# A root by reciprocal and Sqrt in place of Ln and Exp, and a modulation split between ScalarE and VectorE, in a four-norm decoder step

## The chip, the cores and the metric

One core of a Trainium2 chip runs the kernel. The metric is the device time of one execution in microseconds; several executions give a median. The profile shows one execution, whose span runs from its first to its last instruction.

## The reference

One inference step of a small decoder: a prompt of 256 tokens and 8 sequences of 4 sample tokens (288 columns in all), model width 1024, two layers. Each layer has two sublayers, each of which begins with the same modulated norm:

```python
def rms_norm(x, g):
    y = xf * lax.rsqrt(jnp.mean(xf * xf, axis=-1, keepdims=True) + RMS_EPS)
    return (y * g).astype(x.dtype)
def modulate(x, g, shift, scale):
    return rms_norm(x, g) * (1 + scale) + shift
...
x += gate * f(modulate(x, ...))     # f: mixer, SwiGLU, pooling mixer, top-2-of-8 MoE
```

Layer 0 has a mixer (attention with forget gates beside an RWKV-7 recurrence) and a dense SwiGLU; layer 1 has a pooling mixer and a mixture of 8 experts. The recurrence's output passes a group norm per head, `(y - mean) * rsqrt(var + GN_EPS)`, before the output projection. Shift, scale and gate come from a conditioning vector through the matrices called ada below; they differ between the prompt (one vector) and the eight sample sequences (one each).

## The kernel before, in words

Everything is float32 and held transposed: the 1024 features lie as 8 chunks of 128 partitions, the tokens along the columns, prompt in 0 to 255 (NP = 256), samples in 256 to 287. `xT`, `hT`, `tmpT` and `yT` (8 chunks x 288 columns each) are parts of one tensor, which the profile calls `wide`.

Each engine runs its own program in the order in which it is written, and semaphores join them. A modulated norm, number i = 0 to 3, goes like this:

- ScalarE squares the 8 chunks of x (`square_all(i)`); TensorE sums them over the partitions with a matrix of ones (`mean_square(i)`), so that each partition holds the sum for each token.
- VectorE, in `mean_of(i)`, turns the sum into mean + eps in `rstd` (128 x 288, line L1864) and gives the semaphore `ms_read`. ScalarE, in `root(i)` by `inverse_root`, takes Ln (L1611) and Exp with a scale of -0.5 (L1612), and gives `rooted`. VectorE then multiplies all of x by `rstd` into `hT` (L1866, 128 x 2304).
- VectorE, in `modulated(i)`, scales and shifts the sample columns in two operations (L1874, L1875, 128 x 256 each) and then the prompt columns chunk by chunk, 8 operations of 128 x 256 with the chunk's gain and shift as one value per partition (L1878). Each of the eight gives one count of `h_ready`.
- TensorE waits for the chunks one by one: norm 0 before the input projection, norm 1 before the SwiGLU's first gate matrix, norm 3 before the router. Norm 2 is used by VectorE (a copy into `ext`, L2197, and the window sums), by GpSimd and by TensorE, which all wait for its 8 chunks.

In norm 0 the mean and the multiply by `rstd` come early on VectorE, while TensorE still works on the first four ada matrices; the gain and shift (`mod_tile`, `gains(0)`) come later, and `modulated(0)` after them.

The group norm uses the same `inverse_root` on 128 x 1152: three operations of VectorE write variance + eps into `tmpT` (L2138), ScalarE takes Ln and Exp, and VectorE multiplies (L2142), scales and shifts (L2145), adds a bonus (L2146) and multiplies by a gate (L2148), whose end gives `mix_ready`, for which the output projection and the loads of the next weights wait.

Functions of ScalarE belong to table sets. Where the next function is in another set than the one loaded, the build puts an ACT_TABLE_LOAD ahead of it. The other uses of `inverse_root` (q and k norm, the recurrence's key norm) stay as they are.

Of the kernel before, what the change touches and what calls it, by code (L numbers as in the profile page):

```python
# [20 lines left out]
ALU = mybir.AluOpType  # L21
ACT = mybir.ActivationFunctionType
# [3 lines left out]
D = 1024  # L26
DC = D // P
NP, NB, NT = 256, 8, 4
NS = NB * NT
N = NP + NS  # L30
# [3 lines left out]
HC = HW // P  # L34
# [131 lines left out]
class Named:  # L166
# [5 lines left out]
    def __call__(self, name):  # L172
        if name not in self.made:
# [5 lines left out]
ONCE = {  # L179
    "vector": ("vec_copied vec2_copied k_ready q_ready last_ready rp_mixed lf_abs lf_one logf_ready negF_ready "  # L180
              "kk_scaled rk_ready cum_ready psm_shifted psm_ready delta_ops packed final_state gn_centred "
              "mix_ready exts_zero ext_done picked top_ready placed planned numbered weighted y2 y0 y1"),
    "scalar": ("siluc c_copied qk_squared qk_rooted lf_exp lf_ln wl_tanh gl_sigmoid kk_squared kk_rooted "
              "psm_exped so_copied fst_copied syt_copied gn_squared gn_rooted gate_spread top_exped scaled2 scaled0 scaled1"),
    "tensor": ("c_turned vec_turned vec2_turned lf_turned last_turned so_mm fst_mm syt_mm route_mm rank_mm"),
# [39 lines left out]
def spread(ap, axis, n):  # L225

    ap = ap.unsqueeze(axis)
    shape = list(ap.shape)
    shape[axis] = n
    return ap.to_broadcast(shape)  # L230


def flat(t):
    return t[:, :, :].rearrange("p a b -> p (a b)")
# [46 lines left out]
def build_program(nc, a, y_p, y_s, k_p, k_s, v_p, v_s, lf_p, lf_s, st_p, st_s, sh_p, sh_s, pool_p, pool_s):  # L281

    ctx = ExitStack()
    with ctx:
# [3 lines left out]
        s = Named(nc, ctx)  # L288
        once = Once(s)

        def sums(name, which, n):

            return s(f"sums_{which}"), 3 * ("kks", "bon", "gnm", "gnv").index(name) + n
# [236 lines left out]
            return first, out  # L530

        cumv = winv

        def sample_operands():

# [570 lines left out]
        def _(pe):  # L1106
# [67 lines left out]
            for i, (_, wd, chunks) in enumerate(WIN):  # L1174
                w = tile(TILES.index(("win", i)))[:, 0:DC * wd].rearrange("p (c f) -> p c f", c=DC)
                for kind, idx, off, m in chunks:
                    b = banks.open(pe, f"win{n}", (s("win_act" if n % 2 else "win_dve"), n // 2 + 1))
                    for c in range(DC):
                        if n == 0:
                            pe.wait_ge(s("h_ready"), c + 1)  # L1180
                        last = mm(b[0:m, 0:N], w[:, c, off:off + m], hT[:, c, :], c == 0, c == DC - 1)
                    last.then_inc(s("win_mm"), 1)
                    n += 1
                if i == 2:
                    pe.wait_ge(s("vec2_loaded"), 16 * len(others))
                    b = banks.open(pe, "vec2", once("vec2_copied"))
                    for k in range(2):
                        last = pe.transpose(b[:, P * k:P * (k + 1)], vrow[:, 1 + k, :], ident)
                    last.then_inc(once.give("vec2_turned"), 1)
                if i == 4:  # L1190
                    pe.wait_ge(*once("qk_squared"))
                    for k in range(6):
                        b = banks.open(pe, f"qkms{k}", (s("qkms_read"), k + 1))
                        mm(b[:, 0:384], K("pairs"), flat(tmpT)[:, 384 * k:384 * (k + 1)], True, True).then_inc(s("qkms"), 1)
                if i:
                    fold(0, 3 + i)
                ada(0, 4 + i)
# [278 lines left out]
            def hidden(i):  # L1476
                nf = FGRP[i][1]
                for j in range(nf // P):
                    for kind in ("gate", "up"):
                        w = tile(TILES.index((kind, i)))[:, 0:DC * nf].rearrange("p (c f) -> p c f", c=DC)  # L1480
                        n = 4 * i + j
                        b = banks.open(pe, f"{kind}{n}", (s("act_ready"), n + 1))
                        for c in range(DC):
                            if i + j == 0 and kind == "gate":
                                pe.wait_ge(s("h_ready"), DC + c + 1)
                            last = mm(b[:, 0:N], w[:, c, P * j:P * (j + 1)], hT[:, c, :], c == 0, c == DC - 1)
                        last.then_inc(s(f"{kind}_mm"), 1)

# [30 lines left out]
                last = pe.transpose(b[:, 120 * c:120 * (c + 1)], prow[0:120, P * (4 + c):P * (5 + c)], ident[0:120, 0:120])  # L1519
            last.then_inc(s("pb_mm"), 1)  # L1520

            pe.wait_ge(s("h_ready"), 3 * DC)
            for half in range(2):
                b = banks.open(pe, f"hl{half}", (s("hl_copied"), half + 1))
                for c in range(4):
# [25 lines left out]
            for blk, (t0, w) in enumerate(BLK):  # L1551
                for c in range(DC):
                    if blk == 0:
                        pe.wait_ge(s("h_ready"), 3 * DC + c + 1)
                    last = mm(b[0:w, NE * blk:NE * (blk + 1)], hT[:, c, t0:t0 + w], routerw[:, c, :], c == 0, c == DC - 1)
            last.then_inc(once.give("route_mm"), 1)
            for n in range(6):
# [27 lines left out]
        def _(act):  # L1585
# [23 lines left out]
            def inverse_root(v, sem):  # L1609

                me.step(act.activation(v, v, ACT.Ln), chain)  # L1611
                me.give(act.activation(v, v, ACT.Exp, scale=-0.5), sem)  # L1612

            def root(i):
                act.wait_ge(s("ms_read"), i + 1)
                inverse_root(rstd[:, :], s("rooted"))

            square_all(0)
            root(0)
# [1 line left out]
            def ada(layer, i):  # L1621
                k = 12 * layer + i
                act.wait_ge(s("ada_mm"), k + 1)
                if k >= 2:
                    act.wait_ge(s("folded"), k - 1)
                copy(adap[layer][:, k % 2, :], banks[f"ada{layer}_{i}"][:, :], s("ada_copied"))

            for i in range(4):
                ada(0, i)

            def proj_chunk(n):
                kind, idx, _, m = WCHUNKS[n]
# [136 lines left out]
            copy(yT[:, HC:2 * HC, NP:N], banks["syt"][:, 0:HC * NS].rearrange("p (c t) -> p c t", c=HC), once.give("syt_copied"))  # L1769
            act.wait_ge(*once("gn_centred"))  # L1770
            me.give(act.activation(flat(tmpT)[:, 0:HC * N], flat(yT)[:, HC * N:2 * HC * N], ACT.Square), once.give("gn_squared"))  # L1771
            act.wait_ge(*sums("gnv", "read", 3))
            inverse_root(flat(tmpT)[:, 0:HC * N], once.give("gn_rooted"))


            square_all(1)
            root(1)
            for n in range(FF // P):
                act.wait_ge(s("gate_mm"), n + 1)
                if n >= 2:  # L1780
                    act.wait_ge(s("act_ready"), n - 1)
                me.give(act.activation(ffsilu[:, n % 2, :], banks[f"gate{n}"][:, 0:N], ACT.Silu), s("silu_ready"))
                if n >= 4 and (n % 4 == 3 or n == FF // P - 1):
                    ada(1, 2 * (n // 4) - 2)
                    ada(1, 2 * (n // 4) - 1)
# [4 lines left out]
            for half in range(2):  # L1790
                act.wait_ge(s("pb_mm"), half + 1)
                act.wait_ge(*once("exts_zero"))
                me.give(act.activation(exts[:, 4 * half:4 * half + 4, :, 1:16],
                                       banks[f"pb{half}"][:, 0:480].rearrange("p (c b r) -> p c b r", c=4, r=PBUF),
                                       ACT.Copy), s("pbuf_copied"))
            for half in range(2):
                act.wait_ge(s("hl_mm"), half + 1)
                copy(hlast[0:NS + 16, 512 * half:512 * (half + 1)], banks[f"hl{half}"][0:NS + 16, :], s("hl_copied"))
# [6 lines left out]
                copy(dst[0:w, 512 * (n % 2):512 * (n % 2 + 1)], banks[f"gr{n}"][0:w, :], s("hl_copied"))  # L1805
            square_all(3)
            root(3)
            act.wait_ge(*once("ext_done"))
            for n in range(6):
                w = BLK[n // 2][1]  # L1810
# [19 lines left out]
        def _(dve):  # L1830
# [4 lines left out]
            def do(ins, sem=None):  # L1835
                me.step(ins, sem or chain)
# [24 lines left out]

            def mean_of(i):
                dve.wait_ge(s("ms_ready"), i + 1)
                do(TS(rstd[:, :], banks[f"ms{i}"][:, 0:N], 1.0 / D, RMS_EPS, ALU.mult, ALU.add), s("ms_read"))  # L1864
                dve.wait_ge(s("rooted"), i + 1)
                do(TT(hT[:, :, :], xT[:, :, :], spread(rstd[:, :], 1, DC), ALU.mult))  # L1866

            def by_seq(ap):
                return ap.rearrange("p c (b t) -> p c b t", t=NT)

            def modulated(i):

                hs = by_seq(hT[:, :, NP:N])
                do(TT(hs, hs, spread(gainT[i][:, :, 1:9], 3, NT), ALU.mult))  # L1874
                do(TT(hs, hs, spread(mod(i, 0)[:, :, 1:9], 3, NT), ALU.add))  # L1875
                for c in range(DC):
                    v = hT[:, c, 0:NP]
                    me.give(TS(v, v, gainT[i][:, c, 0:1], mod(i, 0)[:, c, 0:1], ALU.mult, ALU.add), s("h_ready"))  # L1878

# [256 lines left out]
            for i in range(3):  # L2136
                dve.wait_ge(*sums("gnv", "mm", i + 1))
                do(TS(flat(tmpT)[:, 384 * i:384 * (i + 1)], banks[f"gnv{i}"][:, 0:384], 1.0 / DH, GN_EPS, ALU.mult, ALU.add),  # L2138
                   s("sums_read"))
            dve.wait_ge(*once("gn_rooted"))  # L2140
            r = flat(tmpT)[:, 0:HC * N]
            do(TT(y2, y2, r, ALU.mult))  # L2142
            for c in range(HC):
                v = yT[:, HC + c, :]
# [48 lines left out]
            do(dve.memset(ext[:, :, 0:16], 0.0))  # L2193
            mean_of(2)
            modulated(2)
            dve.wait_ge(s("h_ready"), 3 * DC)
            do(dve.tensor_copy(ext[:, :, 16:16 + NP], hT[:, :, 0:NP]))  # L2197
            for lv in range(4):
                a0, a1 = (ext, ext2) if lv % 2 == 0 else (ext2, ext)
# [44 lines left out]
        def _(pool):  # L2244
# [93 lines left out]
            pool.wait_ge(s("mix_stored"), 16 * len(stores))  # L2338
            me.step(pool.memset(tables, 0.0), once.give("tables_zero"))

            pool.wait_ge(s("h_ready"), 3 * DC)
            pool.wait_ge(s("pbuf_copied"), 2)
            hs = by_sequence(hT[:, :, NP:N])
            me.step(pool.tensor_copy(exts[:, :, :, 16:20], hs), s("pool_chain"))
# [137 lines left out]
```

## Time and profile before

| | |
|---|---|
| median of 3 runs | 2011.12 us (2007.43 to 2011.98) |
| the profiled execution | 2009.45 us, span 2007.6 us |
| TensorE matmuls busy | 1770.9 us, 88% of the span |
| VectorE, ScalarE, GpSimd busy | 424.8, 241.3, 167.3 us |
| ACT_TABLE_LOADs ahead of L1611 and L1612 | 7 and 7, 1283 ns each |

The busy share of an engine is over the whole span; what a change in one place is worth is read from the engines' rows around that place. In the rows, "idle before" is the time an engine stood still before an instruction, and the arrow names what ended it.

### The profile page before, as it was taken

What the parts mean: (1) busy time and instruction counts of PE and PEld (TensorE: products, weight loads), DVE (VectorE), ACT (ScalarE), POOL (GpSimd) and SP (SyncE); (2) the same over time, 40 slices, a digit from 0 to 9 for tenths busy, and PEclk for the clock granted to TensorE, in tenths of its full rate; (3) what the DMA queues carried; (4) which work ended last, traced back from release to release, by engine and by line L of the source; (5) the groups of instructions that cost most, each with busy time, mean ns of one, the idle gap of its engine ahead of it and who ended that gap; (6) DMA issues with size and microseconds to landing.
All of it is one profiled execution on the core that took longest, in us unless ns stands there. A gap on an engine that the chain in (4) does not pass through costs nothing.

```text
span 2007.6 us, 27180 instructions
## 1 busy us (share of the span) xinstructions
PE 1770.9 (88%) x10676; PEld 1295.1 (65%) x10677; DVE 424.8 (21%) x794; ACT 241.3 (12%) x489; POOL 167.3 (8%) x201
## 2 busy tenths in 40 slices
PE   6999886566789999967889999999999999999874
PEld 3766444555567777745339789788777887778331
DVE  2023435965211111275000000000000000000102
ACT  2022242111110000132000000001000010000101
POOL 4002203562000000040000000000000000000001
PEclk8999597666899999978999999999999999999997
DMA  9762042000745554530898868869999999999995
GB/s 342 269 231 88 2 127 57 1 1 27 249 169 210 210 189 159 190 133 2 315 391 325 304 252 319 302 252 354 363 345 345 346 348 352 343 348 367 367 392 211
DMA packets 235294, 481.64 MB, mean 240 GB/s; under 512 B 16575, under 2 KB 90691, under 8 KB 234803
## 3 DMA queue, kind: packets, MB, share of 16 engines
q1 hardware_dynamic: 229755, 471.92, 65.2%
q0 software_dynamic: 3904, 5.44, 0.9%
q10 hardware_dynamic: 1568, 3.34, 0.5%
q8 instruction: 48, 0.79, 0.2%
q14 instruction: 19, 0.16, 0.0%
HBM read 473.13 MB, written 7.90 MB: 240 GB/s over the span
## 4 chain that ended last, share of the span: by engine, by line
PE 78%; DMA 7%; DVE 5%; POOL 4%; issue 3%; ACT 2%; SPq 2%; ACTq 0%; POOLq 0%; DVEq 0%
PE bank L1108 76%; DMA ring<-in_moe_w_up 4%; POOL ring L2301 2%; DMA ring<-in_ada_w 1%; POOL other L2310 1%; ACT ring L1590 1%; SPq L2423 1%; SPq L2388 0%; DVE wide L1882 0%; DVE wide L1866 0%; PE bank L1241 0%; SPq L2414 0%; DVE wide L2204 0%; PE bank L714 0%; DMA ring<-in_cache_fox_logf 0%
## 5 line engine op out<-in xcount | busy, mean ns | idle before, releaser
L1108 PE MATMUL bank<-wide,ring 128*128 128x144 f32 (+4 forms) x4240 | 695.6, 331 | 16.6 <-DVE wide L1878 9.3
L1108 PEld LDWEIGHTS bank<-wide,ring 128*128 128x128 f32 (+2 forms) x4240 | 616.5, 191 | 100.3 <-issue 34.9
L1108 PE MATMUL bank<-ring 128*64 128x512 f32 (+8 forms) x1748 | 339.3, 519 | 50.6 <-DMA ring<-in_moe_w_up 24.5
L1108 PE MATMUL bank<-other,ring 128*128 128x144 f32 (+3 forms) x2016 | 292.2, 320 | 50.3 <-POOL ring L2301 29.8
L1108 PEld LDWEIGHTS bank<-other,ring 128*128 128x128 f32 (+1 forms) x2016 | 267.8, 194 | 75.3 <-POOL ring L2301 31.4
L1108 PEld LDWEIGHTS bank<-ring 128*64 128x64 f32 (+4 forms) x1748 | 143.1, 158 | 226.2 <-issue 189.2
L1108 PE MATMUL bank<-ring,other 128*64 128x512 f32 x560 | 128.0, 596 | 8.4 <-ACT other L747 8.4
L820 DVE TENSOR_TENSOR other<-other,bank 64x512 f32<-64x512 f32 (+1 forms) x40 | 24.5, 613 | 441.6 <-ACT other L744 441.6
L838 DVE TENSOR_TENSOR other<-other,bank 128x288 f32<-128x288 f32 (+3 forms) x48 | 21.4, 446 | 350.9 <-PE bank L1108 324.4
L2367 POOL TENSOR_TENSOR small<-const 128x1 f32<-128x1 f32 x1 | 0.2, 193 | 1074.7 <-DMA expert_rows<-ring 1074.7
L1108 PEld LDWEIGHTS bank<-ring,other 128*64 128x64 f32 x560 | 38.4, 137 | 75.4 <-issue 64.3
L1108 PEld LDWEIGHTS bank<-const,other 64*128 64x128 f32 (+2 forms) x408 | 49.3, 182 | 32.3 <-issue 28.2
L744 ACT ACTIVATE other<-bank 64x512 f32<-64x512 f32 (+1 forms) x40 | 21.6, 540 | 394.8 <-PE bank L1108 382.9
L2301 POOL TENSOR_TENSOR ring<-ring,const 64x256 f32<-64x256 f32 x48 | 63.7, 1327 | 55.0 <-DVE ring L2095 46.9
L1590 ACT ACTIVATE ring<-bank 128x512 f32<-128x512 f32 (+8 forms) x110 | 45.0, 436 | 166.6 <-PE bank L1108 114.0
L757 ACT ACTIVATE other<-bank 128x288 f32<-128x288 f32 (+3 forms) x48 | 19.3, 403 | 360.9 <-PE bank L1108 349.0
L1108 PE MATMUL bank<-const,other 64*128 64x64 f32 (+2 forms) x408 | 59.0, 281 | 0.0
L1108 PE MATMUL bank<-ring,silucT 128*32 128x512 f32 x384 | 46.6, 616 | 5.0 <-DMA ring<-in_ada_w 5.0
L1108 PE MATMUL bank<-other 128*128 128x288 f32 (+3 forms) x128 | 43.2, 482 | 5.4 <-DVE other L963 2.6
L1590 ACT ACTIVATE other<-bank 128x512 f32<-128x512 f32 (+4 forms) x48 | 24.3, 525 | 171.4 <-PE bank L1108 149.3
L2165 DVE TENSOR_TENSOR other<-other,bank 128x288 f32<-128x288 f32 x22 | 10.0, 454 | 163.1 <-PE bank L1108 163.1
L1108 PE MATMUL bank<-wide,const 128*128 128x288 f32 (+1 forms) x100 | 36.4, 509 | 7.6 <-ACT wide L1771 3.2
(353 smaller groups left out, 956.5 us busy)
## 6 DMA issues: line engine op xcount, KB each, us to landing
ring<-in_moe_w_gate SPq DMA_DIRECT2D x32, 2048.0 KB, 8.0
ring<-in_moe_w_up SPq DMA_DIRECT2D x32, 2048.0 KB, 12.7
ring<-in_moe_w_down SPq DMA_DIRECT2D x32, 2048.0 KB, 16.8
ring<-in_ada_w SPq DMA_DIRECT2D x24, 2048.0 KB, 13.7
ring<-in_moe_w_gate SPq DMA_DIRECT2D x32, 1536.0 KB, 11.1
ring<-in_moe_w_up SPq DMA_DIRECT2D x32, 1536.0 KB, 14.8
ring<-in_moe_w_down SPq DMA_DIRECT2D x32, 1536.0 KB, 16.5
ring<-in_w_in SPq DMA_DIRECT2D x5, 2048.0 KB, 12.7
```

Source lines behind the costliest of these rows:

```text
L744: act.activation(sg[0:HALF, part, 0:P * n], B[part][HALF:P, 0:P * n], ACT.Silu).then_inc(s("moe_silu"), 2)
L757: act.activation(sg[:, p % 2, 0:w], B[2 * (p % 2)][:, 0:w], ACT.Silu).then_inc(s("moe_silu"), 3 if p == 3 else 1)
L820: dve.tensor_tensor(ea[0:HALF, part, 0:P * n], sg[0:HALF, part, 0:P * n], B[part][0:HALF, 0:P * n], ALU.mult)\
L838: dve.tensor_tensor(eaT[:, 2 * p:2 * p + n, 0:k], sg[:, p % 2, 0:n * k].rearrange("p (c q) -> p c q", c=n), B[2 * (p % 2) + 1][:, 0:n * k] ...
L1108: return pe.matmul(out, lhsT, rhs, start=start, stop=stop, skip_group_check=True)
L1590: me.give(act.activation(out, in_, ACT.Copy), sem)
L2165: do(TT(ffact[:, i % 2, n % 4, :], ffsilu[:, n % 2, :], banks[f"up{n}"][:, 0:N], ALU.mult), s("act_ready"))
L2301: me.step(pool.tensor_tensor(nm[o, n % 2], of(gt[o, n % 2], a_)[:, :, 0:L], mask, ALU.mult), s("nm_ready") if a_ else s("pool_chain"))
L2310: me.step(pool.tensor_tensor(vk, spread(sval[:, t, :], 2, DH), spread(svec[:, t, 3, :], 1, 32), ALU.mult), s("vk_ready"))
L2367: me.step(pool.tensor_tensor(small[:, 50:51], ident[:, 0:1], ident[:, 0:1], ALU.add), s("pool_chain"))
L2423: sp.dma_start(svec[2 * H * q + f:2 * H * (q + 1):2].rearrange("p t i k -> p (t i) k"), scratch[q].rearrange("t i h k -> h (t i) k")).then ...
```

## The change

The diff does three things. In the norms and in the group norm, VectorE takes the reciprocal of mean + eps (or variance + eps) and ScalarE one Sqrt of it; `ms_read` and the new `gn_inverted` are given by the reciprocal. The multiply of x by `rstd` leaves `mean_of` and goes into `modulated`, where it is cut into three: the sample columns, the prompt columns of chunks 0 to 3 (whose end gives `h_scaled`), those of chunks 4 to 7. And ScalarE, in its own `modulated(i)`, scales and shifts the prompt columns of chunks 0 to 3 (Identity with the gain as scale and the shift as bias), while VectorE does chunks 4 to 7. TensorE, VectorE and GpSimd wait for `h_act` or `h_ready` through `modulated_chunk`.

```diff
+        HALF_C = DC // 2
+        def modulated_chunk(i, c):
+            return (s("h_act"), HALF_C * i + c + 1) if c < HALF_C else (s("h_ready"), HALF_C * i + c + 1 - HALF_C)
...
-                            pe.wait_ge(s("h_ready"), c + 1)
+                            pe.wait_ge(*modulated_chunk(0, c))
...
             def root(i):
                 act.wait_ge(s("ms_read"), i + 1)
-                inverse_root(rstd[:, :], s("rooted"))
+                me.give(act.activation(rstd[:, :], rstd[:, :], ACT.Sqrt), s("rooted"))
+            def modulated(i):
+                for c in range(HALF_C):
+                    act.wait_ge(s("h_scaled"), i + 1)
+                    v = hT[:, c, 0:NP]
+                    act.activation(v, v, ACT.Identity, scale=gainT[i][:, c, 0:1], bias=shift_of(i)[:, c, 0:1]).then_inc(s("h_act"), 1)
...
-            act.wait_ge(*sums("gnv", "read", 3))
-            inverse_root(flat(tmpT)[:, 0:HC * N], once.give("gn_rooted"))
+            act.wait_ge(*once("gn_inverted"))
+            me.give(act.activation(flat(tmpT)[:, 0:HC * N], flat(tmpT)[:, 0:HC * N], ACT.Sqrt), once.give("gn_rooted"))
...
             def mean_of(i):
                 dve.wait_ge(s("ms_ready"), i + 1)
-                do(TS(rstd[:, :], banks[f"ms{i}"][:, 0:N], 1.0 / D, RMS_EPS, ALU.mult, ALU.add), s("ms_read"))
+                do(TS(rstd[:, :], banks[f"ms{i}"][:, 0:N], 1.0 / D, RMS_EPS, ALU.mult, ALU.add))
+                do(dve.reciprocal(rstd[:, :], rstd[:, :]), s("ms_read"))
                 dve.wait_ge(s("rooted"), i + 1)
-                do(TT(hT[:, :, :], xT[:, :, :], spread(rstd[:, :], 1, DC), ALU.mult))
...
             def modulated(i):
                 hs = by_seq(hT[:, :, NP:N])
+                do(TT(hT[:, :, NP:N], xT[:, :, NP:N], spread(rstd[:, NP:N], 1, DC), ALU.mult))
                 do(TT(hs, hs, spread(gainT[i][:, :, 1:9], 3, NT), ALU.mult))
                 do(TT(hs, hs, spread(mod(i, 0)[:, :, 1:9], 3, NT), ALU.add))
-                for c in range(DC):
+                for c0, sem in ((0, s("h_scaled")), (HALF_C, chain)):
+                    do(TT(hT[:, c0:c0 + HALF_C, 0:NP], xT[:, c0:c0 + HALF_C, 0:NP], spread(rstd[:, 0:NP], 1, HALF_C), ALU.mult), sem)
+                for c in range(HALF_C, DC):
                     v = hT[:, c, 0:NP]
                     me.give(TS(v, v, gainT[i][:, c, 0:1], mod(i, 0)[:, c, 0:1], ALU.mult, ALU.add), s("h_ready"))
...
+            r = flat(tmpT)[:, 0:HC * N]
+            do(dve.reciprocal(r, r), once.give("gn_inverted"))
             dve.wait_ge(*once("gn_rooted"))
-            r = flat(tmpT)[:, 0:HC * N]
             do(TT(y2, y2, r, ALU.mult))
```

ScalarE's `modulated(0)` stands after its copies for the first four ada matrices, `modulated(1)` and `modulated(3)` right after their `root`, `modulated(2)` after `root(2)` and two copies into `exts`.

## Rows read from the trace of the kernel before

**Rows 1.** The page's chain that ended last, shares of the span by engine
```profile
PE 78%; DMA 7%; DVE 5%; POOL 4%; issue 3%; ACT 2%; SPq 2%; ACTq 0%; POOLq 0%; DVEq 0%
```

**Rows 2.** Waits of TensorE, 44 to 120 us: total, times, longest
```profile
PE bank L1108 <- DVE wide L1878: 2.3, 1, 2.3
```

**Rows 3.** Windows: stretch, length, busy (instructions) of PE, PEld, DVE, ACT, POOL, clock, DMA
```profile
45.50:50.00 4.50, 4.46 (x10) 3.21 (x11) 2.15 (x7) 0.00 (x0) 0.00 (x0) 0.50 1.05 387
...
560.00:854.00 294.00, 294.00 (x1357) 220.07 (x1358) 42.27 (x109) 19.29 (x41) 0.00 (x0) 0.99 0.51 183
```

**Rows 4.** Timeline, norm 1: start, duration, engine, line, operation, [idle before, releaser]
```profile
552.91 0.46 DVE L1864 TENSOR_SCALAR rstd<-bank 128x288 f32<-128x288 f32 x1 [2.95 <-PE bank L1108]
553.40 0.44 ACT L1611 ACTIVATE rstd<-rstd 128x288 f32<-128x288 f32 x1 [1.66 <-DVE rstd L1864]
553.86 1.28 ACT L1612 ACT_TABLE_LOAD   x1
555.15 0.44 ACT L1612 ACTIVATE rstd<-rstd 128x288 f32<-128x288 f32 x1
...
555.70 2.56 DVE L1866 TENSOR_TENSOR wide<-wide,rstd 128x2304 f32<-128x2304 f32 x1 [2.33 <-ACT rstd L1612]
...
559.21 2.67 DVE L1878 TENSOR_SCALAR wide<-wide,gainT,modT 128x256 f32<-128x256 f32 x8
...
559.77 6.47 PE L1108 MATMUL bank<-wide,ring 128*128 128x288 f32 x18 [6.97 <-DVE wide L1878]
```

**Rows 5.** Timeline, the group norm's root
```profile
505.71 0.56 DVE L2138 TENSOR_SCALAR wide<-bank 128x384 f32<-128x384 f32 x1 [0.72 <-PE bank L1108]
...
508.78 1.16 ACT L1612 ACTIVATE wide<-wide 128x1152 f32<-128x1152 f32 x1
510.04 1.36 DVE L2142 TENSOR_TENSOR wide<-wide 128x1152 f32<-128x1152 f32 x1 [3.77 <-ACT wide L1612]
```

**Rows 6.** Timeline, norm 0 (VectorE), and TensorE's first projection matmuls
```profile
26.12 2.56 DVE L1866 TENSOR_TENSOR wide<-wide,rstd 128x2304 f32<-128x2304 f32 x1 [2.33 <-ACT rstd L1612]
...
44.06 0.42 DVE L1874 TENSOR_TENSOR wide<-wide,gainT 128x256 f32<-128x256 f32 x1
...
45.54 18.73 PE L1108 MATMUL bank<-wide,ring 128*128 128x288 f32 x64 [2.32 <-DVE wide L1878]
```

**Rows 7.** Timeline, norms 2 and 3 and the router
```profile
859.43 2.56 DVE L1866 TENSOR_TENSOR wide<-wide,rstd 128x2304 f32<-128x2304 f32 x1 [2.33 <-ACT rstd L1612]
...
865.65 1.23 DVE L2197 COPY other<-wide 128x2048 f32<-128x2048 f32 x1
...
893.78 2.56 DVE L1866 TENSOR_TENSOR wide<-wide,rstd 128x2304 f32<-128x2304 f32 x1 [2.33 <-ACT rstd L1612]
...
897.85 7.92 PE L1108 MATMUL bank<-routerw,wide 128*128 128x8 f32 x48 [6.97 <-DVE wide L1878]
```

**Rows 8.** Small VectorE operations: ns min/median/max, first and last start, shapes
```profile
L1986 DVE RECIPROCAL small<-small x8: 165/166/166, 203.0 to 239.5; 128x2 f32<-128x2 f32 x8
...
L1063 DVE RECIPROCAL low<-low x1: 176/176/176, 935.5 to 935.5; 128x3 f32<-128x3 f32 x1
...
L1040 DVE TENSOR_SCALAR low<-low x1: 153/153/153, 927.4 to 927.4; 128x1 f32<-128x1 f32 x1
...
L994 DVE TENSOR_TENSOR low<-low x1: 159/159/159, 918.0 to 918.0; 128x1 f32<-128x1 f32 x1
```

**Rows 9.** ScalarE by form: busy us, mean ns, idle before; then a timeline row
```profile
L1590 ACT ACTIVATE other<-bank 128x288 f32<-128x288 f32 x17 | 7.0, 410 | 92.2 <-PE bank L1108 92.2
...
L1693 ACT ACTIVATE other<-bank,vT 128x288 f32<-128x288 f32 x8 | 4.0, 498 | 3.0 <-PE bank L1108 3.0
...
L1800 ACT ACTIVATE silucT<-modT 128x256 f32<-128x256 f32 x1 | 0.4, 403 | 0.0
...
16.88 2.77 ACT L1607 ACTIVATE wide<-wide 128x288 f32<-128x288 f32 x8 [6.09 <-DVE wide L1842]
```

**Rows 10.** Timeline, ScalarE's first copy for the experts after the top-2 Exp
```profile
924.07 0.41 ACT L946 ACTIVATE wide<-bank 128x288 f32<-128x288 f32 x1 [7.03 <-PE bank L1108]
```

More of the change, by code:

```diff
@@ L181 @@
               "kk_scaled rk_ready cum_ready psm_shifted psm_ready delta_ops packed final_state gn_centred "
-              "mix_ready exts_zero ext_done picked top_ready placed planned numbered weighted y2 y0 y1"),
+              "gn_inverted mix_ready exts_zero ext_done picked top_ready placed planned numbered weighted y2 y0 y1"),
     "scalar": ("siluc c_copied qk_squared qk_rooted lf_exp lf_ln wl_tanh gl_sigmoid kk_squared kk_rooted "
@@ L532, in build_program, with shift_of @@
         cumv = winv
+        HALF_C = DC // 2
+        def shift_of(i):
+            return modT[i // 2][:, 24 * (i % 2):24 * (i % 2) + 8, :]
+        def modulated_chunk(i, c):
+            return (s("h_act"), HALF_C * i + c + 1) if c < HALF_C else (s("h_ready"), HALF_C * i + c + 1 - HALF_C)
         def sample_operands():
@@ L1484, in hidden @@
                             if i + j == 0 and kind == "gate":
-                                pe.wait_ge(s("h_ready"), DC + c + 1)
+                                pe.wait_ge(*modulated_chunk(1, c))
                             last = mm(b[:, 0:N], w[:, c, P * j:P * (j + 1)], hT[:, c, :], c == 0, c == DC - 1)
@@ L1520, in _ @@
             last.then_inc(s("pb_mm"), 1)
-            pe.wait_ge(s("h_ready"), 3 * DC)
+            for c in (HALF_C - 1, DC - 1):
+                pe.wait_ge(*modulated_chunk(2, c))
             for half in range(2):
@@ L1553, in _ @@
                     if blk == 0:
-                        pe.wait_ge(s("h_ready"), 3 * DC + c + 1)
+                        pe.wait_ge(*modulated_chunk(3, c))
                     last = mm(b[0:w, NE * blk:NE * (blk + 1)], hT[:, c, t0:t0 + w], routerw[:, c, :], c == 0, c == DC - 1)
@@ L1629, in _ @@
                 ada(0, i)
+            modulated(0)
             def proj_chunk(n):
@@ L1771, in _ @@
             me.give(act.activation(flat(tmpT)[:, 0:HC * N], flat(yT)[:, HC * N:2 * HC * N], ACT.Square), once.give("gn_squared"))
-            act.wait_ge(*sums("gnv", "read", 3))
-            inverse_root(flat(tmpT)[:, 0:HC * N], once.give("gn_rooted"))
+            act.wait_ge(*once("gn_inverted"))
+            me.give(act.activation(flat(tmpT)[:, 0:HC * N], flat(tmpT)[:, 0:HC * N], ACT.Sqrt), once.give("gn_rooted"))
             square_all(1)
             root(1)
+            modulated(1)
             for n in range(FF // P):
@@ L1795, in _ @@
                                        ACT.Copy), s("pbuf_copied"))
+            modulated(2)
             for half in range(2):
@@ L1807, in _ @@
             root(3)
+            modulated(3)
             act.wait_ge(*once("ext_done"))
@@ L2195, in _ @@
             modulated(2)
-            dve.wait_ge(s("h_ready"), 3 * DC)
+            for c in (HALF_C - 1, DC - 1):
+                dve.wait_ge(*modulated_chunk(2, c))
             do(dve.tensor_copy(ext[:, :, 16:16 + NP], hT[:, :, 0:NP]))
@@ L2339, in _ @@
             me.step(pool.memset(tables, 0.0), once.give("tables_zero"))
-            pool.wait_ge(s("h_ready"), 3 * DC)
+            for c in (HALF_C - 1, DC - 1):
+                pool.wait_ge(*modulated_chunk(2, c))
             pool.wait_ge(s("pbuf_copied"), 2)
```

## The prediction, as it was put on record

> **What bounds the kernel now.** First the page's chain of work that ended last: 78% of it is TensorE [rows 1], so the norms matter only where TensorE stands still for them. The question for each of the five places that the diff touches (norms 0 to 3, the group norm) is whether the wait there ends last and whether the time is given back later. The waits of TensorE and the timeline answer it. At norm 0 TensorE waits 2.3 us for the first modulated chunk and for nothing else up to 120 us [rows 2], so what is lost there is lost for the projections. At norm 1 it stands still for 6.97 us, and the reader can follow the baton: VectorE's mean, Ln, a table load, Exp, the multiply, two sample operations, the first chunk [rows 4]. After that it works without a gap from 560 to 854 us [rows 3], so no transfer takes the difference up. The group norm's root is the 3.77 us for which VectorE waits while TensorE waits too [rows 5]. Norm 2 feeds VectorE's own chain of window sums, and norm 3 the router, before which TensorE again stands for 6.97 us [rows 7]. All five are on the path, except the first half of norm 0: its multiply ends at 28.68 us, while its gains are ready only at 44.06 [rows 6].
>
> **What is removed.** Ln and Exp cost, from the end of the mean (553.37) to the start of the multiply (555.70), 2.33 us: 0.03 to reach ScalarE, 0.44 Ln, 0.02, a table load of 1.28, 0.44 Exp, 0.11 back [rows 4]. Ln's own load is not in it: ScalarE stood idle for 1.66 us just before Ln, with its table already in. Sqrt takes Ln's place and its load can hide in the same idle time, so I count none for it. The same stretch of the group norm is 3.77 us [rows 5].
>
> On the load, the Trainium skill (ScalarE: Activation LUTs, What ACT_TABLE_LOAD costs) says that a switch costs the 1.28 us load plus a drain of about 1.38. The trace does not show that drain: the load starts 0.02 us after Ln ends, and Exp 0.01 after the load [rows 4]. By the page, four switches off the path would give back 5.5 us more than the rows allow, an estimate that turns a sum of +9.2 into +3.7; it gets no chance of its own, because the rows time this very switch.
>
> **What is added in its place: a reciprocal.** Write r for its time per column in ns and take 0.15 us as its fixed part. The new stretch of a norm is 0.03 + (0.15 + 0.288 r) + 0.03 + 0.44 + 0.11 = 0.76 + 0.288 r, against 2.33: a change of -1.57 + 0.288 r. The group norm: 0.03 + (0.15 + 1.152 r) + 0.03 + 1.16 + 0.10 = 1.47 + 1.152 r against 3.77: -2.30 + 1.152 r. Norms 1, 2 and 3 and the group norm together: -7.0 + 2.02 r. Norm 0's root is covered by the 15 us that VectorE has until its gains; if that cover went, it would cost as much as the others.
>
> So everything hangs on r, and no reciprocal of more than three columns is in the trace. Lower end: the rate of ordinary operations, (2558 - 159) / 2303 = 1.04 ns a column, from the multiplies of 2304 columns and of one [rows 4, 8]. Upper end: two reciprocals of different width, 166 ns at two columns and 176 at three, 10 ns a column [rows 8]. In between: if the fixed part is that of the one-column tensor-scalar (153 less its column, 152), two columns give 7 and three give 8 ns. One column more or less is thin evidence, since fixed parts vary by some nanoseconds from operation to operation; but at the ordinary rate the step from two columns to three should be 1 ns and is 10. I take r = 8, near the steep rows. Then the reciprocal is 2.45 us in a norm and 9.4 in the group norm, and the roots together cost -7.0 + 16.1 = +9.1 us: the norms +0.73 each, the group norm +6.9.
>
> The Trainium skill (VectorE: DVE Perf Modes, First, the fixed hardware budget) says that the reciprocal is an iterative divide on two slices with a repeat count of 8; at that page's 0.96 GHz, if the count is paid per column, that is 8.3 ns, an estimate by which the sum would be +9.9 us instead of the +9.2 below.
>
> **What is moved: the multiply and the split.** After the root, before: multiply, two sample operations (0.46 each with the gap), first chunk, and TensorE starts 4.07 us after the multiply's start in norms 1 and 3 [rows 4, 7]. After: three sample operations, 3 x 0.46 = 1.38; half the prompt, 0.16 + 1024 x 1.04 ns = 1.23, and 0.04 to reach ScalarE; one Identity; 0.14 to TensorE, as now. An Identity of 256 columns with two per-partition operands is not in the trace: a copy of that size takes 0.403, one per-partition operand adds 0.088 (498 against 410 at 288 columns) [rows 9]; with a second, 0.58, taken as 0.60. The first chunk is then there at 3.4 us.
>
> - Norm 1: 3.4 against 4.07, -0.67. At the half clock that TensorE has after such a pause, a matmul takes 0.45 us (ten in 4.46 at granted clock 0.50 [rows 3]). Squares of 288 columns follow each other at 0.33 though one lasts 0.44 [rows 9], so Identities should follow at 0.33 to 0.60, say 0.45: they keep up. At 0.60, three chunks lose 0.45.
> - Norm 0: the multiply now stands behind the gains. Before, 44.06 to 45.54 = 1.48; after, 3.4: +1.92 on the path [rows 6]. This cover is what the edit gives up.
> - Norm 2: VectorE needs all chunks itself, before 865.65 - 859.43 = 6.22 [rows 7]; after, 1.38 + two halves 2.53 + four chunks at 0.33 and a last tail, 1.45 = 5.36: -0.86. ScalarE's four are done by 2.65 + 0.60 + 3 x 0.45 = 4.6, earlier.
> - Norm 3: the router takes a chunk in about 0.33 (24 chunk products of two parts in 7.92 [rows 7]), so ScalarE's pace shows. Before, the first 8 were through at 4.07 + 8 x 0.33 = 6.71; after, 3.4 + 3 x 0.45 + 5 x 0.33 = 6.40: -0.31, between -0.67 and +0.14.
>
> Together +0.08, within -0.4 and +1.0: the split nearly pays for norm 0.
>
> **Costed at nothing.** The top-2 softmax's Exp now finds Sqrt's table and needs its own load, 1.28; ScalarE stands idle for 7.03 us behind it [rows 10], so nothing is late. SwiGLU's Silu load moves behind four Identities; ScalarE has nothing to do until the first gate product, 8 matmuls of 0.36 us or more after TensorE's start [rows 4]. Identity may need a table of its own; its load would fall in the time that ScalarE waits for `h_scaled`. `ms_read` comes later by the reciprocal, and with it a PSUM bank that is next taken eight banks on. No DMA issue is moved; SP's loads after `mix_ready` shift with it.
>
> **Sum.** -7.0 + 16.1 + 0.1 = +9.2 us on the profiled execution's 2009.45 (span 2007.6 and 1.85 around it), 2018.65. The median of the runs is 1.67 above that execution, so the forecast is 2011.12 + 9.2 = 2020.3. In general the sum is -6.9 + 2.02 r: it is zero at r = 3.4, and 0.2% (4.0 us, about what a measurement of this kernel can tell from no change) is passed above 5.4 and below 1.4.
>
> **Rivals.**
> 1. The reciprocal runs at one column a cycle, like the rest. For it: all other VectorE operations do, and 166 against 159 ns at so few columns is no great difference. Against it: the 10 ns step. Then the sum is -6.9 + 2.1 = -4.8, 2006.3 us: faster, by just over 0.2%. It decides wherever r is below 1.4. Chance 0.21. The Trainium skill (Vector Engine (DVE) Microarchitecture Reference, ALU special-value part) has the divide chain span all eight slices, which a pipeline could feed with a column a cycle; no row here shows that.
> 2. A rate between, 2 to 5 ns: 2008.3 to 2014.3 us, no change to be told. For it: fixed part 158, as the one-column multiply has [rows 8], gives 4 and 6. Chance 0.08.
> 3. Sqrt's load is not hidden: it lands behind the wait at the group norm and at norm 2 (norms 1 and 3 find it loaded), +2.6 us on the forecast, 2022.9. Against it: Ln's load, in the same place, was early. Chance 0.03.
> 4. The forecast, r from 5.4 to 10: 2015 to 2025, with the split's bounds. Chance 0.68.
>
> **Range and chances.** The likeliest case has 2015 to 2025.5 for itself. It holds too little alone, so the range goes down to rival 1's time: 2006 to 2025.5, leaving out half of rival 1 and the ends. Slower 0.71 (forecast and rival 3), same 0.16 (rival 2 and the part of rival 1 that falls short of 0.2%), faster 0.13.
>
> **What would show it.** The RECIPROCAL rows of 288 and 1152 columns: 2.45 and 9.4 us here, 0.46 and 1.36 in rival 1. VectorE's idle before the first multiply after a root: 0.60 us instead of 2.33. No table load between the reciprocal and Sqrt. TensorE's start after the gains of norm 0: 3.4 us instead of 1.48; the first Identity 0.60 long. The prediction is wrong if a 288-column reciprocal is under 1.7 us.

## The result, and the profile after

The changed kernel takes 2018.07 us (median of 8 runs, 2014.45 to 2019.70), the kernel before 2010.77 beside it (8 runs, 2007.41 to 2013.45). The medians lie 7.3 us apart. The ratio with its 95% interval, which is the measure from here on, is 1.0028 [1.0015, 1.0040]: slower by 5.6 us (3.0 to 8.0), against a forecast of +9.2 (2020.3 us). The profiled execution took 2018.64 us, its span 2016.8, against 2009.45 and 2007.6.

Line numbers move: L1864 of before is L1886, Ln and Exp of a norm (L1611, L1612) have become the reciprocal L1887 and Sqrt L1627, the first chunks' scale and shift is ScalarE's L1634, and the group norm's multiply L2142 is L2168. VectorE by form, grouped by line (busy us, mean ns of one, idle before), after:

```profile
L1887 DVE RECIPROCAL rstd<-rstd 128x288 f32<-128x288 f32 x4 | 7.8, 1953 | 0.1
L2166 DVE RECIPROCAL wide<-wide 128x1152 f32<-128x1152 f32 x1 | 7.4, 7353 | 0.0
L2011 DVE RECIPROCAL small<-small 128x2 f32<-128x2 f32 x8 | 1.3, 166 | 0.3
L1073 DVE RECIPROCAL low<-low 128x3 f32<-128x3 f32 x1 | 0.2, 175 | 0.0
```

The two wide rows give the unknown of the prediction: (7353 - 1953) / 864 = 6.25 ns a column, and 1953 - 288 x 6.25 = 153 ns fixed. That line passes through the two-column row too (165.5 against 166).

Timeline of norm 1, after, which answers to [rows 4]:

```profile
561.10 0.46 DVE L1886 TENSOR_SCALAR rstd<-bank 128x288 f32<-128x288 f32 x1 [2.95 <-PE bank L1118]
561.59 1.95 DVE L1887 RECIPROCAL rstd<-rstd 128x288 f32<-128x288 f32 x1
563.58 0.44 ACT L1627 ACTIVATE rstd<-rstd 128x288 f32<-128x288 f32 x1 [4.95 <-DVE rstd L1887]
564.12 0.43 DVE L1896 TENSOR_TENSOR wide<-wide,rstd 128x256 f32<-128x256 f32 x1 [0.58 <-ACT rstd L1627]
564.58 0.42 DVE L1897 TENSOR_TENSOR wide<-wide,gainT 128x256 f32<-128x256 f32 x1
565.04 0.42 DVE L1898 TENSOR_TENSOR wide<-wide,modT 128x256 f32<-128x256 f32 x1
565.50 2.48 DVE L1900 TENSOR_TENSOR wide<-wide,rstd 128x1024 f32<-128x1024 f32 x2
566.76 1.58 ACT L1634 ACTIVATE wide<-wide,modT,gainT 128x256 f32<-128x256 f32 x3 [2.74 <-DVE wide L1900]
...
567.50 0.82 PE L1118 MATMUL bank<-wide,ring 128*128 128x288 f32 x1 [6.51 <-ACT wide L1634]
```

No table load stands between reciprocal and Sqrt. From the end of the mean (561.56) to the first multiply (564.12) it is 2.56 us where [rows 4] have 2.33: the root lost 0.23. From there to TensorE's start it is 3.38 where it was 4.07: the split won 0.69. TensorE stands still for 6.51 us instead of 6.97.

Timeline of the group norm's root, after, for [rows 5]:

```profile
504.24 1.28 ACT L1792 ACT_TABLE_LOAD   x1
...
508.25 0.56 DVE L2163 TENSOR_SCALAR wide<-bank 128x384 f32<-128x384 f32 x1 [0.38 <-PE bank L1118]
508.84 7.35 DVE L2166 RECIPROCAL wide<-wide 128x1152 f32<-128x1152 f32 x1
516.23 1.16 ACT L1792 ACTIVATE wide<-wide 128x1152 f32<-128x1152 f32 x1 [10.70 <-DVE wide L2166]
517.49 1.36 DVE L2168 TENSOR_TENSOR wide<-wide 128x1152 f32<-128x1152 f32 x1 [1.30 <-ACT wide L1792]
...
523.55 1.81 PE L1118 MATMUL bank<-wide,other 128*128 128x288 f32 x3 [15.41 <-DVE wide L2174]
```

The load runs while VectorE still waits for the sums. From the end of the last variance to the multiply it is 517.49 - 508.81 = 8.68 us, against 3.77: +4.91, and TensorE waits 15.41 us for the whole chain (10.50 before). This is the largest single loss.

VectorE's timeline, after: first operations behind the gains (norm 0) and behind the roots of norms 2 and 3, for [rows 6, 7]:

```profile
42.43 0.23 DVE L1882 TENSOR_TENSOR gainT<-gainT,vT 128x72 f32<-128x72 f32 x1
42.70 0.42 DVE L1896 TENSOR_TENSOR wide<-wide,rstd 128x256 f32<-128x256 f32 x1
...
868.00 0.42 DVE L1896 TENSOR_TENSOR wide<-wide,rstd 128x256 f32<-128x256 f32 x1 [0.58 <-ACT rstd L1627]
...
873.38 1.23 DVE L2224 COPY other<-wide 128x2048 f32<-128x2048 f32 x1
...
901.75 0.43 DVE L1896 TENSOR_TENSOR wide<-wide,rstd 128x256 f32<-128x256 f32 x1 [0.58 <-ACT rstd L1627]
```

And TensorE's, after: the first projection matmuls, the router, and what follows it:

```profile
46.08 4.18 PE L1118 MATMUL bank<-wide,ring 128*128 128x288 f32 x8 [4.22 <-ACT wide L1634]
...
905.13 8.05 PE L1118 MATMUL bank<-routerw,wide 128*128 128x8 f32 x48 [6.52 <-ACT wide L1634]
913.11 4.84 PE L1572 MATMUL bank<-const,wide 128*128 128x128 f32 x24
...
923.52 6.79 PE L1118 MATMUL bank<-other 128*128 128x288 f32 x27 [1.00 <-DVE other L973]
```

Norm 0 starts the projections 46.08 - 42.70 = 3.38 us behind its gains, 1.90 later than before (1.48). The copy into `ext` starts 5.38 us after the multiply (6.22 before), the router 3.38 (4.07 before).

One table for the whole span, in us: each stretch runs from the milestone before it. "Unchanged" is the kernel before run once more (below).

| stretch | before | unchanged | after | changed again |
|---|---|---|---|---|
| start to gains of norm 0 | 44.02 | 42.80 | 42.66 | 42.38 |
| to the projections' start | 1.52 | 1.52 | **3.42** | **3.42** |
| to the group norm's mean | 453.08 | 453.84 | 455.08 | 451.39 |
| to its multiply | 11.42 | 11.43 | **16.33** | **16.33** |
| to the output projection's start | 6.06 | 6.06 | 6.06 | 6.06 |
| to norm 1's mean | 36.81 | 38.29 | 37.55 | 37.76 |
| to the first gate matmul | 6.86 | 6.86 | **6.40** | **6.40** |
| to norm 2's mean | 296.87 | 297.62 | 297.48 | 297.58 |
| to the copy into `ext` | 9.01 | 9.02 | **8.40** | **8.41** |
| to norm 3's mean | 25.34 | 25.33 | 25.34 | 25.34 |
| to the router's start | 6.86 | 6.87 | **6.41** | **6.41** |
| to the top-8 search | 8.36 | 8.36 | **8.49** | **8.49** |
| to the experts' plan | 21.38 | 21.75 | 22.49 | 22.55 |
| to the experts' first matmul | 25.33 | 25.49 | 25.16 | 25.34 |
| to the end | 1054.68 | 1054.76 | 1055.53 | 1055.54 |

The bold stretches are the edited places. They sum to +1.90 + 4.91 - 0.46 - 0.61 - 0.45 + 0.13 = +5.4 us, and they repeat to 0.01 us. The rest of the 9.2 between the two spans lies in stretches that also differ by up to 1.5 us between the two executions of the unchanged kernel, and by 3.7 (to the group norm's mean) between those of the changed one: run to run, except for the stretch to the plan, which is taken up below.

### The profile page after: what moved, and what is told of

Same layout as the page of the kernel before. It is cut to its first block, busy times and chain, and to the rows that moved or that the text cites. A ratio compares the mean times of both kernels' runs of the same rounds, so it can differ in the third digit from the quotient of the medians.

```text
span 2016.8 us, 27183 instructions
## 1 busy us (share of the span) xinstructions
PE 1774.4 (88%) x10676; PEld 1296.4 (64%) x10677; DVE 436.2 (22%) x791; ACT 239.3 (12%) x494; POOL 167.5 (8%) x201
## 4 chain that ended last, share of the span: by engine, by line
PE 77%; DMA 6%; DVE 6%; POOL 3%; issue 3%; SPq 2%; ACT 2%; ACTq 0%; DVEq 0%; POOLq 0%
PE bank L1118 76%; DMA ring<-in_moe_w_up 4%; POOL ring L2328 2%; DMA ring<-in_ada_w 1%; POOL other L2337 1%; ACT ring L1601 1%; SPq L2451 1%; SPq L2416 0%; DVE wide L1907 0%; DVE wide L2166 0%; PE bank L1251 0%; DVE wide L2231 0%; SPq L2442 0%; DMA ring<-in_cache_fox_logf 0%; DVE wide L1900 0%
## 5 line engine op out<-in xcount | busy, mean ns | idle before, releaser
L848 DVE TENSOR_TENSOR other<-other,bank 128x288 f32<-128x288 f32 (+3 forms) x48 | 21.4, 446 | 350.9 <-PE bank L1118 324.8
```

Source lines behind the costliest of these rows:

```text
L848: dve.tensor_tensor(eaT[:, 2 * p:2 * p + n, 0:k], sg[:, p % 2, 0:n * k].rearrange("p (c q) -> p c q", c=n), B[2 * (p % 2) + 1][:, 0:n * k] ...
```

## The experiments

Theories, stated for all runs: **A**, the reciprocal's rate per column is the whole loss, and the edited rows add up to the time. **B**, the rival: the split, or something behind the rows (ScalarE's pace, the clock of TensorE), takes a share that the rows of the edited places don't show. Ratios are against the kernel before on the same chip, five rounds each, its median beside them.

### Roots alone, and the split alone

```diff
# e1_roots_only: the kernel before, and
-                inverse_root(rstd[:, :], s("rooted"))
+                me.give(act.activation(rstd[:, :], rstd[:, :], ACT.Sqrt), s("rooted"))
...
+                do(dve.reciprocal(rstd[:, :], rstd[:, :]), s("ms_read"))
...   # the same in the group norm
# e2_split_only: the kernel after, with inverse_root in both places and no reciprocal
```

> Reciprocal and Sqrt in the four norms and the group norm, but no split: VectorE multiplies and modulates all chunks as before. If the reciprocals make the loss (1.95 us at 288 columns and 7.35 at 1152 in the profile after), each norm is +0.23 us (0.76 + 1.80 - 2.33) in norms 1 to 3 and the group norm +4.9 (1.47 + 7.20 - 3.77): +5.6 us over the kernel before, about 2016.4. If the loss comes from the split and the moved multiply, this kernel is within 2 us of the one before.

Measured: 2020.08 us against 2010.09, 1.0048 [1.0030, 1.0065]. Its rows: norms 1 to 3 +0.23 each, the group norm +4.94, norm 0 nothing (its projections start 1.52 us after the gains, as before), +5.6 in all. The time says +9.6 (6.0 to 13.1), 4.0 more than the rows.

> The split between ScalarE and VectorE and the moved multiply, but all roots by Ln and Exp as before. Reciprocal theory: norm 0 +1.9, norms 1 to 3 together -1.9 (-0.67, -0.86, -0.31 were forecast), so no change from the kernel before, within 1 us. Split theory: +5 us or more over before.

Measured: 2011.24 against 2010.09, 1.0009 [0.9998, 1.0021]. Its rows: norm 0 +1.90, norms 1 to 3 -0.69, -0.83 and -0.55, together -0.2. The time says +1.8 (-0.4 to +4.2), 2.0 above the rows, which the interval does not resolve. So the loss sits in the roots, as A has it; the excess of e1 over its rows is open.

### The group norm's reciprocal, taken away, doubled, and alone

```diff
# e3_gn_undone: the kernel after, but
-            do(dve.reciprocal(r, r), once.give("gn_inverted"))
...
+            inverse_root(flat(tmpT)[:, 0:HC * N], once.give("gn_rooted"))
# e4_gn_twice: the kernel after, and ahead of its own reciprocal
+            do(dve.reciprocal(flat(tmpT)[:, HC * N:2 * HC * N], r))
# e8_gn_only: the kernel before, and
+            do(dve.reciprocal(r, r), once.give("gn_inverted"))   # and one Sqrt for Ln and Exp
```

> The whole change, except that the group norm's root is Ln and Exp again. Reciprocal theory: 4.9 us faster than the whole change, so +0.8 over before (three norms +0.7, split +0.1). If the group norm's extra time is given back later (the loads after it have more time), it stays within 1.5 us of the whole change, +6 to +7 over before.

Measured: 2013.79 against 2010.09, 1.0020 [1.0009, 1.0030]; the stretch to the group norm's multiply is 11.40 us again, where the kernel after has 16.33. The other edited rows leave +0.5, and the time says +4.0 (1.8 to 6.0), 3.5 above them. That is neither of the two times expected: +0.8 lies outside the interval, and +6 at its edge.

> The whole change with a second reciprocal of 1152 columns into a scratch part ahead of the group norm's own; no result changes. If the time of that instruction passes to the end one to one, +7.35 us over the whole change, about +14 over before. If what follows takes part of it back, less than +5 over the whole change.

Measured: 2024.94 against 2010.09, 1.0077 [1.0062, 1.0092], +15.5 (12.5 to 18.5), 9 to 10 us above what the ratios of the kernel after give (+5.6, and +6.4 below), where +7.35 was expected; the intervals hold that too. VectorE's timeline of it:

```profile
508.58 7.35 DVE L2166 RECIPROCAL wide<-wide 128x1152 f32<-128x1152 f32 x1
515.97 7.35 DVE L2167 RECIPROCAL wide<-wide 128x1152 f32<-128x1152 f32 x1
```

The second copy costs its 7.35 us and the 0.04 between them, all on the path: the stretch to the group norm's multiply is 23.66 us instead of 16.33, and nothing covers the reciprocal. Its edited rows add up to +12.8, and the time lies 2.7 above them.

These four kernels were timed beside one and the same group of runs of the kernel before, and all four lie above their rows, by 4.0, 2.0, 3.5 and 2.7 us. Compared with each other, e4 and e3, which differ in the group norm's root alone, are 11.5 us apart by their ratios and 12.3 by their rows. An offset that the four have in common drops out of that difference, and the two reciprocals show in it nearly whole.

> The kernel before with one edit, the group norm's root by reciprocal and Sqrt. Per-column theory (0.15 us + 6.25 ns a column, 7.35 us at 1152): 1.47 + 7.20 against 3.77, +4.9 us, ratio 1.0024, which is most of the whole change's loss. If the loss is spread over the norms or lies in the split, under +2.

Measured: 2015.93 against 2010.96, 1.0023 [1.0012, 1.0034], +4.6 (2.4 to 6.8), where its one edited stretch has +4.86. Here rows and time agree.

### How large the noise is

The kernel before and the kernel after were run once more (c1_unchanged, c2_changed_again).

> The kernel before once more, as a measure of what two runs of one program differ by, in total and in each stretch between the norms: ratio 1.000 within 0.001 by any theory. If stretches that no edit touches (projection start to group norm, output projection, top-2 to plan) come out 1 to 2 us longer here too than in the first profile of before, their difference in the other kernels is not the change's.

> The changed kernel once more, beside the runs of this chip. The sum over the rows of its edited places is +5.1 us (norm 0 +1.9, group norm +4.6, norms 1 to 3 -1.4); the first timing gave +7.3 between medians. Rows theory: +5 to +6. If the change costs another 2 us in stretches that it doesn't edit: +7 to +8.

Measured: 2010.02 against 2010.91, 0.9996 [0.9985, 1.0007]; and 2015.61, 1.0032 [1.0020, 1.0044], +6.4 (4.0 to 8.8). The second agrees with the result, and its interval holds both theories of its expectation (whose +5.1 counted 4.6 for the group norm; the rows have 4.91). What differs beyond the edited rows shows in TensorE's windows (length, busy and matmuls, granted clock, DMA share, GB/s) of the router and of the transposes behind it; unchanged kernel first, then after:

```profile
899.70:907.50 7.80, 7.80 (x49) 0.50 0.00 0
907.50:911.90 4.40, 4.40 (x28) 0.62 0.01 4
```

```profile
905.10:913.10 8.00, 7.97 (x48) 0.50 0.00 0
913.10:917.90 4.80, 4.80 (x28) 0.57 0.01 3
```

TensorE comes out of its wait at a granted clock of 0.50 (1.2 GHz) in both. In the kernel after it stays there for longer in the transposes, 4.84 us for 24 of them against 4.09 and 4.46 in the two executions of the unchanged kernel. VectorE waits for a matmul behind them before it goes on to the plan; its timeline, unchanged kernel first, then after:

```profile
913.85 0.17 DVE L969 COPY low<-bank 128x8 f32<-128x8 f32 x1 [3.44 <-PE bank L1108]
```

```profile
919.86 0.17 DVE L979 COPY low<-bank 128x8 f32<-128x8 f32 x1 [3.82 <-PE bank L1118]
...
924.88 0.17 DVE L995 COPY low<-const 128x8 f32<-128x8 f32 x1 [0.33 <-issue]
```

The wait is 3.82 us instead of 3.06 (in the first execution of before) and 3.44. And VectorE stands still at L995 for 0.33 us for which the profile shows no cause ("issue"); neither execution of the unchanged kernel has that gap. Together they make the stretch to the plan +0.7 to +1.1 us.

### Norm 0 given back, and the roots given back

```diff
# e5_norm0_early: the kernel after, but norm 0 multiplies in mean_of and VectorE does its 8 chunks
+                if i == 0:
+                    do(TT(hT[:, :, :], xT[:, :, :], spread(rstd[:, :], 1, DC), ALU.mult))
...
-                for c in range(HALF_C, DC):
+                for c in range(HALF_C if i else 0, DC):
# e6_lnexp_split123: e5 with inverse_root in both places
```

> The whole change, but in norm 0 the multiply stays early on VectorE and VectorE does all 8 chunks, as before; the split stands in norms 1 to 3 alone. Norm 0's start after the gains goes from 3.42 back to 1.52 us, so 1.9 us faster than the whole change, if that loss passes to the end. If TensorE makes up for a late start in norm 0 later, no difference.

Measured: 2015.55 against 2010.91, 1.0026 [1.0015, 1.0036]. The projections start 1.52 us after the gains again, so norm 0's 1.90 us are back on the rows. The time shows 1.2 less than its neighbour c2 (1.0026 against 1.0032), which the intervals don't resolve.

> The parts that the rows call a gain: all roots by Ln and Exp as before, norm 0 as before, the split in norms 1 to 3. Rows theory: -0.69, -0.83 and -0.55 us, -2.1 us against the kernel before, ratio 0.999. Rival: the split costs something outside of the norms that the rows of the norms don't show, then 0 to +2 us.

Measured: 2010.76 against 2010.91, 1.0001 [0.9991, 1.0012]. The edited rows are -2.07 us (norms 1 to 3 by the split), and the stretch to the plan 22.82 instead of 21.38 to 21.75. TensorE's windows of it, the router and the transposes:

```profile
896.92:904.90 7.98, 7.98 (x48) 0.50 0.00 0
904.90:910.20 5.30, 5.30 (x28) 0.52 0.01 3
```

Over half of what the split wins goes back there: the router starts 0.69 us sooner after the mean, and its transposes run almost wholly at half clock (5.32 us for the 24). The time, +0.2 (-1.8 to +2.4), is what the rival expected (0 to +2), and with that stretch counted the rows come to -0.6 to -1.0, which the interval holds.

### A narrow root

If the width is what the reciprocal costs, it could be made narrow: one value per token on 128 partitions, 3 columns instead of 288, spread back by TensorE.

```diff
# e7_narrow_root: e6, and in norms 1 to 3
+ for blk, t0 in enumerate((0, P, N - P)):
+     last = mm(b[:, 8 * blk:8 * blk + 8], tmpT[:, c, t0:t0 + P], K("ones")[:, 0:8], c == 0, c == DC - 1)
...
+ do(TS(rcol[:, :], banks[f"ms{i}"][:, 0:24:8], 1.0 / D, RMS_EPS, ALU.mult, ALU.add))
+ do(dve.reciprocal(rcol[:, :], rcol[:, :]), s("ms_read"))
...
+ last = mm(b[:, t0:t0 + w], rcol[:, blk:blk + 1].to_broadcast([P, P]), ident[:, P - w:P], True, True)
```

> Reciprocal and Sqrt kept in norms 1 to 3, but on 3 columns: the mean squares are summed with the tokens on the partitions (three 128-token blocks), so that VectorE and ScalarE work on 128 x 3, and three matmuls against the identity spread the roots over all partitions again. Group norm and norm 0 as before, split in norms 1 to 3. Per-column theory: the reciprocal falls from 1.95 to about 0.18 us, the root from VectorE's mean to the multiply takes about 1.5 us with the three matmuls, against 2.33 + 0.46 before: 0.9 to 1.2 us less in each of three norms, with the split's 2.1 some 5 us faster than before by rows, 2006. If a reciprocal costs a fixed amount whatever its width, or the extra matmuls and hand-overs eat it: within 2 us of before.

Measured: 2014.60 against 2010.96, 1.0018 [1.0009, 1.0026], a miss. In this kernel the mean squares of the prompt tokens leave out one of the eight chunks; the work is the same. TensorE's and VectorE's timelines of norm 1:

```profile
553.38 7.80 PE L1121 MATMUL bank<-const,wide 128*128 128x8 f32 x48
562.04 1.46 PE L1121 MATMUL bank<-const,rcol 128*128 128x128 f32 x6 [0.86 <-ACT rcol L1647]
566.99 5.62 PE L1121 MATMUL bank<-wide,ring 128*128 128x288 f32 x11 [3.48 <-ACT wide L1654]
```

```profile
561.29 0.16 DVE L1906 TENSOR_SCALAR rcol<-bank 128x3 f32<-128x3 f32 x1 [6.71 <-PE bank L1121]
561.49 0.17 DVE L1907 RECIPROCAL rcol<-rcol 128x3 f32<-128x3 f32 x1
```

The reciprocal is down to 0.17 us and the way from the mean to the first gate matmul to 5.70 (6.86 before). But the sums take 48 small matmuls of 7.80 us, and VectorE waits 6.71 us for them where it waited 2.95 [rows 4]: the gain is more than spent ahead of the place that was mended.

### One function in place of both

What the edited places pay for is a second operation in the root. ScalarE has a function for the whole of it.

```diff
# e10_one_function: the kernel before, in root(i) and, the same, in the group norm
-                inverse_root(rstd[:, :], s("rooted"))
+                me.give(act.activation(rstd[:, :], rstd[:, :], ACT.Abs_reciprocal_sqrt), s("rooted"))
# e9_one_function_split: e6 with the same two lines
```

> The roots of the four norms and the group norm by a single function of ScalarE, 1/sqrt(|x|), with no reciprocal on VectorE and no second table load; norm 0 as before and the split in norms 1 to 3. If one function in one table set takes the time of Ln or Exp alone and its load hides where Ln's did: 0.58 us instead of 2.33 in norms 1 to 3, 1.29 instead of 3.77 in the group norm, -7.7 us, and the split's -2.1 by rows (0 in the timing of the split with Ln and Exp): 2001 to 2004, ratio 0.995 to 0.996. If the function needs two tables or a load behind its wait, 1.28 less gain at each.

> The kernel before with that one function in the four norms and the group norm and nothing else: -7.7 us by the same rows, ratio 0.996; what differs from the kernel with the split as well is the split's worth (rows: 2.1 us).

Measured: e9 2003.41 against 2011.79, 0.9963 [0.9949, 0.9977]; e10 2003.47, 0.9964 [0.9951, 0.9978]. Both beat the kernel before and the kernel after, by 7.2 us (4.4 to 9.9) against before for e10. Its timeline in norm 1 and, ahead of it, in the group norm (VectorE, then ScalarE):

```profile
505.45 1.36 DVE L2142 TENSOR_TENSOR wide<-wide 128x1152 f32<-128x1152 f32 x1 [1.30 <-ACT wide L1773]
...
549.36 0.46 DVE L1864 TENSOR_SCALAR rstd<-bank 128x288 f32<-128x288 f32 x1 [2.95 <-PE bank L1108]
550.39 2.56 DVE L1866 TENSOR_TENSOR wide<-wide,rstd 128x2304 f32<-128x2304 f32 x1 [0.58 <-ACT rstd L1616]
```

```profile
499.55 1.28 ACT L1773 ACT_TABLE_LOAD   x1
504.18 1.16 ACT L1773 ACTIVATE wide<-wide 128x1152 f32<-128x1152 f32 x1 [3.35 <-DVE wide L2138]
...
549.85 0.44 ACT L1616 ACTIVATE rstd<-rstd 128x288 f32<-128x288 f32 x1 [2.96 <-DVE rstd L1864]
```

From mean to multiply it is now 0.58 us instead of 2.33, and 1.30 instead of 3.77 in the group norm: -1.75 x 3 - 2.47 = -7.7 on the rows. The load hides in idle time, as Sqrt's did. No run here compares how exact the function is. With the split on top (e9) the rows give 2.1 more and the time gives nothing that can be told.

## Why the prediction was right, point by point

- **Direction and mechanism: right.** Roots cost, the split pays for norm 0. The roots came to +5.6 us (3 x 0.23 + 4.91), the split to -0.2.
- **The rate r: the mis-sized term.** "I take r = 8, near the steep rows" measured 6.25. That alone is 2.02 x 1.75 = 3.5 us of the forecast's +9.2; the general sum -6.9 + 2.02 r gives +5.7 with it, where the rows add up to +5.4. The step from two columns to three (10 ns), which set the upper end, is 6.25 on the line of the wide rows; the other 4 ns are of the size by which small operations differ anyway (153 and 159 ns for two of one column [rows 8]). The two small rows could not decide the rate: with a fixed part of 152 ns they gave 7 and 8, with 158 they gave 4 and 6, on either side of the 5.4 that divided the forecast from rival 2. That 6.25 fell on the forecast's side was in part luck. Its formulas hold to 0.01 us: 0.76 + 0.288 x 6.25 = 2.56, as measured, and 1.47 + 1.152 x 6.25 = 8.67 against 8.68. The 288-column reciprocal took 1.95 us, not 2.45, the wide one 7.35, not 9.4; the first is above the 1.7 us below which the prediction called itself wrong.
- **Split.** Norm 0 +1.90 (forecast +1.92), norm 1 -0.69 (-0.67), norm 2 -0.84 (-0.86), norm 3 with the router's 0.13 -0.55 (-0.31): ScalarE's pace costs the router less than I thought. One Identity took 589 ns (0.60 taken), and three in 1.58 us are (1.58 - 0.589) / 2 = 0.50 apart (0.45 taken). ScalarE by form, after, grouped by line:

```profile
L1634 ACT ACTIVATE wide<-wide,modT,gainT 128x256 f32<-128x256 f32 x16 | 8.3, 589 | 12.1 <-DVE wide L1900 12.1
...
L1627 ACT ACT_TABLE_LOAD x2 | 2.6, 1283 | 0.0
...
L1802 ACT ACT_TABLE_LOAD x1 | 1.3, 1283 | 0.0
L1841 ACT ACT_TABLE_LOAD x1 | 1.3, 1283 | 0.0
```

- **Costed at nothing: right.** Sqrt's loads, Silu's (L1802) and the top-2 Exp's (L1841) run in time that ScalarE has to spare; behind the last, its idle time before the first copy for the experts falls from 7.03 [rows 10] to 5.59 us. VectorE waits 0.58 us for a root (0.60 forecast).
- **Rival 1 (one column a cycle): refuted**, since 1.95 and 7.35 us are far from its 0.46 and 1.36. **Rival 2** asked for 2 to 5 ns, which 6.25 is not. **Rival 3** (a load behind the wait) is refuted by the group norm's load at 504.24, 12 us ahead of its Sqrt, and norm 2's at 863.19, 4.3 us ahead.
- **What the sum left out.** In the timed runs the excess over the edited rows is small for the kernel after (+5.6 and +6.4 against +5.4). One part of it is located, the stretch to the plan: 21.4 to 21.8 us in the three profiles whose norms 2 and 3 were left alone (before, unchanged, e8), and 22.1 to 23.0 in the eleven that moved them. TensorE's longer time at half clock behind the router makes about half of it or more (in e7 hardly any), and in seven of the eleven VectorE stands still for another 0.2 to 0.35 us near L995. What keeps the clock down there was not settled. Nor was the excess of e1 to e4, 2.0 to 4.0 us, of which this stretch gives 0.7 to 1.6; the rest may belong to what the four share, the runs of before and the chip, but no run here shows it.

On r, the Trainium skill (VectorE: DVE Perf Modes, First, the fixed hardware budget) speaks of an iterative divide with a repeat count of 8, from which I had estimated 8.3 ns a column. The rows do not bear this out: 6.25 ns is six cycles, not eight, at that page's 0.96 GHz.

The Trainium skill (ScalarE: Activation LUTs, What it computes) advises a reciprocal on VectorE followed by a Sqrt for a reciprocal root, and gives accuracy as the reason, which no run here measures. In these rows that form takes 0.23 us more than Ln, a load and Exp at 288 columns, 4.91 more at 1152, and 1.98 and 7.38 more than the single function of e10.

## What to carry to other kernels

An operation that looks like the others in a profile's list can run at another rate per column: price it from two widths far apart, and treat a rate read from two and three columns as a range. Before an operation is moved from one engine to another to save a table load, ask whether a load stands on the path at all and whether one function does the whole step: here one function won 7 us where the exchange lost 6. And work that waits behind a late operand (norm 0's multiply behind the gains) loses the cover that it had, at its full length.

## What was not expected of the hardware

The reciprocal's cost is a straight line from 2 to 1152 columns (within 4 ns), 0.153 us + 6.25 ns a column, six times the 1.04 ns of VectorE's multiplies [rows 4, 8]. And after the pause before the router, 24 transposes took 4.09, 4.27 and 4.46 us in kernels with unedited norms 2 and 3, and 4.48 to 5.38 in the others, though they are the same work: the granted clock of that stretch was 0.62 in the unchanged kernel and 0.52 to 0.57 in two of the others.
